# Column sums of four norms moved ahead of the last chunk that leads to them, the experts' residual inside the last V group, and weights split at other places

## The chip, the cores and the metric

The kernel runs on one core of one Trainium2 chip. The metric is the device time of one execution in microseconds (us). The engines are TensorE (PE; its weight loads are PEld), VectorE (DVE), ScalarE (ACT), GpSimd (POOL) and SyncE (SP), which issues nearly all transfers.

## The reference, cut to what matters

Two layers work on 512 prompt tokens and 32 sample tokens (T = 544) of width 1024:

```python
mod = silu(c) @ w_ada[l] + b_ada[l]               # sh1, sc1, g1, sh2, sc2, g2
h = rmsnorm(x, norm_mix_g[l]) * (1 + sc1) + sh1
y = mix_even(h, ...) if l % 2 == 0 else mix_odd(h, ...)
x = x + g1 * y
h = rmsnorm(x, norm_ffn_g[l]) * (1 + sc2) + sh2
x = x + g2 * peer(h, wq[l], k1[l], k2[l], u[l], v[l])
...
return rmsnorm(x, final_g), ...                   # and the new states
```

`mix_even` (layer 0) runs a GLU, a depthwise convolution with 31 taps, a LayerNorm and a swish over 512 channels, and causal means over 2, 4, 8 and 16 tokens with a linear map over the other 512; both feed one output projection. `mix_odd` (layer 1) is a short gated convolution between two projections. `peer` takes, per token and head, the best 16 of 128 x 128 experts: `sum_k g_k * gelu(u_k . h) * v_k`. The kernel computes gelu(U h) for all 16384 experts and multiplies by gates that are zero where an expert wasn't picked.

## The kernel before, in words

**Layout.** Everything is feature-major. X and H are [128, 8 chunks, 544] in f32. A product in f32 precision is made from f16 halves: each operand is split in a high part and a low part (value minus high part), and three matmuls (high by high, high by low, low by high; `PASSES`) accumulate in f32. A chunk of 128 output features takes 8 x 3 x 2 = 48 matmuls of 272 columns. PSUM is cut into four pairs of banks that are handed round (`begin` waits until the pair's last reader is done); for the first uses only three go round.

**Weights.** A slot of 128 x 4096 f32 comes into `raw[lane]` (two lanes), ACT makes its high part (`high`, L865), DVE its low part (`low`, L1193). Before that, ACT waits for the slot's transfer and until PE is done with every use of PSUM so far, so that `parts[lane]` is free. SP starts the next transfer into the lane when the low part is made.

**A norm.** ACT squares the chunks of X into H; PE multiplies them by a matrix of ones in f32 (`column_sums`, L613: for each chunk one matmul of 512 columns and one of 32, 32 records in all), which gives every partition the sum over features. DVE scales it into `stat` (L1162, `inverse_root`), ACT takes the inverse root (L849), DVE refines it in four steps (L1164 to L1167) and multiplies the eight chunks (L1172, `norm_x`), ACT modulates each (L856, `modulate`), and the result is split for the matmuls: ACT's copy to f16 (L870, `high_part`) and DVE's low part (L1200, `low_part`). ACT does all eight modulations before the eight copies. In norm 0 of layer 0 DVE makes both halves itself, chunk by chunk (L1249, L1251).

There are five norms: 0 at the start, 1 between layer 0's output projection and its queries, 2 between layer 0's experts and layer 1's input projection, 3 as 1 in layer 1, and 4 at the end (no modulation and no split; L1576 writes y). Ahead of norms 1 and 3, `project` (L580) makes eight chunks of the output projection with lane 0 for four and lane 1 for four; DVE adds each to X (`residual`, L1182), ACT squares (L1008).

**Ahead of norm 1, in layer 0.** The rest of `w_ada` is taken beside the input projection: 24 slots, each one call of `ada_rows(s)` on PE (L627, 16 records) into two buffers that the transfers refill (L404), and after every fourth an `ada_turn` (L637). DVE meanwhile does the convolution's 31 taps on two groups of two channel chunks (L1307, one instruction a tap and chunk); within the second group, after tap 10, the window sums, and after tap 24 the low halves of the four pool chunks (L1322) and the low part of lane 0's output weights. Pool chunk 3 takes the PSUM pair that chunk 0 leaves. ACT makes the high part of these weights after `take_rows(5)`, which waits for the last `ada_rows`.

**V phase.** A loop of 16 turns; a turn is two groups of 4 x 128 experts (`v_group`, L732), each eight chunks of 24 matmuls into one pair. DVE adds each chunk to ACC (L1539), and between the adds it splits the next weights and makes the next gated activations. After the last group `residual(l, "g2", True)` adds ACC times the gate to X (two instructions a chunk), and norm 2 or 4 follows. At the start of layer 1 both lanes' weights are split on ACT and DVE between the squares and the norm's first step.

Of the kernel before, what the change touches and what calls it, by code (L numbers as in the profile page):

```python
# [26 lines left out]
ALU = mybir.AluOpType  # L27
# [8 lines left out]
KD = D // P  # L36
# [35 lines left out]
FREE_FROM, LAST_FREE = 9, 14  # L72
CORNER = max(WINDOWS)
# [172 lines left out]
def build(nc, xT, vectors, state_a, state_b, state_c, w_pool, keys, whole_w, split_w, U, V,  # L246
          out_y, out_ap, out_as, out_bp, out_bs, out_cp, out_cs, gates_dram, act_dram, x_dram):
    with ExitStack() as ctx:
# [298 lines left out]
        def _(pe):  # L547
# [68 lines left out]

            def ada_rows(s):
# [104 lines left out]
            def v_group(lane, grp):  # L722

                pe.wait_ge(split[lane], lanes[lane].at(1))
                for c in range(KD):
                    u = begin("dve")
# [8 lines left out]
                    mm.then_inc(mm_done, 1)  # L735
                wts.n += 4
# [4 lines left out]
            for l in range(LAYERS):  # L741
                column_sums(begin("dve"), H, KD, sq_ready, NORM[2 * l] + 1)
                if l == 0:
                    for s in range(EARLY):
                        ada_rows(s)
# [18 lines left out]
                    for g in range(KA):  # L764
                        pool_branch(g)
                    for s in range(20, 2 * ADA_SLOTS):
                        ada_rows(s)
                        if s % 4 == 0:
                            ada_turn(s // 4 - 1)
                    ada_turn(2 * ADA_SLOTS // 4 - 1)  # L770
# [16 lines left out]
                    for m in range(4):  # L787
                        project(begin("dve"), 1, m, range(KD), True, True).then_inc(mm_done, 1)
                else:
# [4 lines left out]
                    for m in range(8):  # L794
# [4 lines left out]
                column_sums(begin("dve"), H, KD, sq_ready, NORM[2 * l + 1] + 1)  # L799
# [24 lines left out]
                with loop(pe, BODIES, *w.steps(dve=16), (lanes[0], 1), (lanes[1], 1), (wts, 8)):  # L824
# [4 lines left out]
            column_sums(begin("dve"), H, KD, sq_ready, NORM[4] + 1)  # L829
# [3 lines left out]
        def _(act):  # L833
# [32 lines left out]

            def high_part(src, dst, semaphore, value, signal):
                for k in range(KD):
                    act.wait_ge(semaphore, value + k)
                    act.copy(dst[:, 0, k, :], src[:, k, :]).then_inc(signal, 1)  # L870
# [51 lines left out]
            for l in range(LAYERS):  # L922
# [12 lines left out]
                else:  # L935
                    squares(X, H, KD, x_ready, 1)
                    for lane in range(2):
                        high(lane, U_SCALE)
                    root()
                    modulate(l, 0)  # L940
                    high_part(H, HM[l], h_ready, 2 * KD * l + 1, hm_high)
                if l == 0:
# [13 lines left out]
                    for g in range(KA):  # L956
                        take_pool(g)
                    take_turn(4)
                    take_rows(5)
                    high(0, 1.0)  # L960
# [41 lines left out]
                for half in range(2):  # L1002
# [134 lines left out]
        def _(dve):  # L1137
# [21 lines left out]
            def inverse_root(n, width):  # L1159

                u = next_use()
                dve.tensor_scalar(stat[:, 0, :], ps(u), 1.0 / width, EPS, ALU.mult, ALU.add).then_inc(dve_read, 1)  # L1162
# [11 lines left out]
            def residual(l, gate, experts):  # L1174
                for k in range(KD):
                    if experts:
                        pieces = [(ACC[:, k, a:b], a, b, s) for a, b, s in SEG]
                    else:
                        v = ps_halves(next_use())
                        pieces = [(v[:, 0, :], 0, HALF, 0), (v[:, 1, 0:NP_ - HALF], HALF, NP_, 0), (v[:, 1, NP_ - HALF:HALF], NP_, T, 1)]  # L1180
                    for y, a, b, s in pieces:
                        ins = dve.scalar_tensor_tensor(out=X[:, k, a:b], in0=y, scalar=mod[:, l, mod_at[gate] * KD + k, s:s + 1],  # L1182
# [468 lines left out]
```

## Time and profile before

| what | value |
|---|---|
| median of three runs | 3772.31 us (3771.55 to 3772.61) |
| profiled execution, its time | 3770.65 us |
| profiled execution, its span | 3768.9 us |
| TensorE's granted clock, mean | 0.983 of full speed |
| PE busy | 3627.0 us, 96% of the span |
| DVE busy | 2586.1 us, 69% |
| ACT busy | 1027.2 us, 27% |

The span is the time from the first to the last instruction of the profiled execution; its own time is 1.75 us more. PE is busy nearly throughout, so what matters are the few stretches where it is not.

### The profile page before, as it was taken

Reading aid. Unit: us, or ns where it says so; the run is one execution under the profiler, and the core shown is the slowest. Engines: PE = TensorE matmul, PEld = TensorE weight load, DVE = VectorE, ACT = ScalarE, POOL = GpSimd, SP = SyncE. Lnnn points to the kernel's source line nnn. Section 1 sums busy time; section 2 is a strip of 40 time slices with the busy share of each in tenths; the row PEclk is TensorE's granted clock in tenths of the full one; section 3 lists DMA queues with packets and bytes.
Section 4 is the critical chain, followed back from the end, with each engine's and each line's share of the span. In section 5 each row is a group of like instructions: output and inputs, shape, how many; then the busy total and the mean of one; then the engine's idle time right before and its main releaser. Section 6 shows DMA issues by size and latency. Waiting matters only on the chain.

```text
span 3768.9 us, 72843 instructions
## 1 busy us (share of the span) xinstructions
PE 3627.0 (96%) x31816; PEld 2959.8 (79%) x31816; DVE 2586.1 (69%) x3938; ACT 1027.2 (27%) x922; POOL 11.9 (0%) x34
## 2 busy tenths in 40 slices
PE   7778999999999999999979899999999999999998
PEld 3357888888888888888845688888888888888886
DVE  4857755556665888888734585555666488888886
ACT  3034333343332111111132333243343411111111
POOL 0000000000000000000000000000000000000000
PEclk9889999999999999999989999999999999999999
DMA  8732245454558454545312213464554775454540
GB/s 339 315 119 76 92 160 193 172 194 174 190 203 312 184 195 192 198 184 197 135 67 90 103 68 137 161 203 158 195 197 167 247 278 198 184 195 187 203 184 35
DMA packets 196225, 667.12 MB, mean 177 GB/s; under 512 B 11952, under 2 KB 151360, under 8 KB 152512
## 3 DMA queue, kind: packets, MB, share of 16 engines
q1 hardware_dynamic: 190608, 663.67, 47.3%
q8 instruction: 159, 2.61, 0.3%
q10 hardware_dynamic: 5392, 0.56, 0.1%
q14 instruction: 34, 0.28, 0.0%
q0 software_dynamic: 32, 0.01, 0.0%
HBM read 514.72 MB, written 149.49 MB: 176 GB/s over the span
## 4 chain that ended last, share of the span: by engine, by line
PE 92%; DVE 4%; DMA 3%; ACT 1%; issue 0%; SPq 0%; DVEq 0%; ACTq 0%
PE PS L732 38%; PE PS L688 35%; PE PS L663 5%; PE PS L600 4%; PE PS L718 3%; PE PS L580 2%; PE PS L613 1%; PE PS L627 1%; DMA ring<-whole_w 1%; DMA arena<-gates_dram 1%; PE PS L676 1%; ACT H L856 1%; DVE ring L1193 1%; PE PS L595 1%; DMA arena<-act_dram 1%; DVE arena L1307 1%
## 5 line engine op out<-in xcount | busy, mean ns | idle before, releaser
L688 PE MATMUL PS<-X,ring 128*128 128x272 f16 x12288 | 1437.0, 279 | 0.0
L732 PE MATMUL PS<-arena,ring 128*128 128x272 f16 x12288 | 1423.7, 279 | 2.6 <-DVE ring L1193 2.6
L732 PEld LDWEIGHTS PS<-arena,ring 128*128 128x128 f16 x12288 | 1202.2, 98 | 224.1 <-issue 3.2
L688 PEld LDWEIGHTS PS<-X,ring 128*128 128x128 f16 x12288 | 1198.8, 98 | 218.7 <-issue 0.4
L1193 DVE SCALAR_TENSOR_TENSOR ring<-ring 128x4096 f16<-128x4096 f32 x149 | 659.0, 4424 | 637.5 <-ACT ring L865 628.9
L865 ACT ACTIVATE ring<-ring 128x4096 f16<-128x4096 f32 x149 | 538.5, 3615 | 1154.8 <-PE PS L732 1119.3
L1539 DVE TENSOR_TENSOR ACC<-PS,ACC 128x544 f32<-128x544 f32 x512 | 363.1, 719 | 236.0 <-PE PS L732 236.0
L1035 ACT ACTIVATE H<-PS 128x544 f32<-128x544 f32 x256 | 159.7, 624 | 974.6 <-PE PS L688 974.5
L1529 DVE TENSOR_TENSOR arena<-arena 128x544 f32<-128x544 f32 x256 | 292.6, 1143 | 45.7 <-DMA arena<-act_dram 45.7
L663 PE MATMUL PS<-X,ring 128*128 128x272 f16 x1536 | 186.4, 282 | 29.4 <-DVE X L1200 29.4
L663 PEld LDWEIGHTS PS<-X,ring 128*128 128x128 f16 x1536 | 149.4, 99 | 63.5 <-issue 35.1
L1533 DVE TENSOR_TENSOR arena<-arena 128x544 f16<-128x544 f32 x256 | 185.8, 726 | 8.7
L600 PE MATMUL PS<-arena,ring 128*128 128x512 f16 (+1 forms) x1152 | 141.4, 279 | 22.0 <-DVE arena L1200 22.0
L600 PEld LDWEIGHTS PS<-arena,ring 128*128 128x128 f16 x1152 | 70.7, 96 | 92.6 <-issue 24.5
L1057 ACT COPY ACC<-PS 128x1024 f32<-128x1024 f32 x136 | 131.4, 1016 | 23.5 <-PE PS L718 23.5
L718 PE MATMUL PS<-arena 128*128 128x128 f16 x2176 | 136.4, 218 | 0.0
L718 PEld LDWEIGHTS PS<-arena 128*128 128x128 f16 x2176 | 130.5, 97 | 2.6
L1482 DVE TENSOR_TENSOR arena<-pairs,arena 128x2048 f16<-128x2048 f16 x68 | 83.1, 1222 | 67.5 <-PE PS L718 67.1
L1531 DVE CAST arena<-arena 128x544 f16<-128x544 f32 x256 | 113.7, 444 | 8.8
L580 PE MATMUL PS<-ACC,ring 128*128 128x272 f16 x768 | 94.0, 286 | 14.4 <-DVE ring L1193 7.1
L580 PEld LDWEIGHTS PS<-ACC,ring 128*128 128x128 f16 x768 | 76.7, 100 | 31.3 <-DVE ACC L1346 7.2
L1307 DVE SCALAR_TENSOR_TENSOR arena<-arena,vec 128x574 f32<-128x574 f32 x120 | 87.7, 814 | 0.0
(149 smaller groups left out, 1538.1 us busy)
## 6 DMA issues: line engine op xcount, KB each, us to landing
ring<-U SPq DMA_DIRECT2D x64, 2048.0 KB, 10.6
ring<-V SPq DMA_DIRECT2D x64, 2048.0 KB, 7.6
act_dram<-H SPq DMA_DIRECT2D x64, 1088.0 KB, 5.0
gates_dram<-ACC SPq DMA_DIRECT2D x68, 1024.0 KB, 5.7
arena<-gates_dram SPq DMA_DIRECT2D x32, 2176.0 KB, 9.5
arena<-act_dram SPq DMA_DIRECT2D x64, 1088.0 KB, 5.0
ring<-split_w SPq DMA_DIRECT2D x17, 2048.0 KB, 9.0
arena<-whole_w SPq DMA_DIRECT2D x11, 2048.0 KB, 10.9
```

What stands on the lines that cost most here:

```text
L580: mm = pe.matmul(ps_halves(u)[:, half, :], parts[lane][:, pw, k * 512 + m * P:k * 512 + (m + 1) * P], Z16[:, ph, k, half * HALF:(half + 1) ...
L600: mm = pe.matmul(ps(u)[:, a:b], parts[lane][:, pw, k * 512 + m * P:k * 512 + (m + 1) * P], HM[l][:, ph, k, a:b], start=(k == n == 0), stop ...
L663: mm = pe.matmul(ps_halves(u)[:, half, :], parts[lane][:, pw, k * 512 + c % 4 * P:k * 512 + (c % 4 + 1) * P], H16[:, ph, k, half * HALF:(h ...
L688: mm = pe.matmul(ps_halves(u)[:, half, :], parts[lane][:, pu, k * 512 + j * P:k * 512 + (j + 1) * P], H16[:, ph, k, half * HALF:(half + 1) ...
L718: mm = pe.matmul(ps(u, 1024)[:, i * P:(i + 1) * P], E2[:, buf, b, :, e], G1[:, buf, n, b, :, e], start=(n == 0), stop=(n == 1))
L732: mm = pe.matmul(ps_halves(u)[:, half, :], parts[lane][:, pv, j * D + c * P:j * D + (c + 1) * P], WT[:, grp, pw, j, half * HALF:(half + 1) ...
L865: act.activation(parts[lane][:, 0, :], raw[lane], ACT.Copy, scale=scale).then_inc(high_made[lane], 1)
L1035: act.activation(dst.rearrange("p (b c) -> p b c", b=2), ps_halves(u), ACT.Gelu_apprx_tanh, scale=1.0 / U_SCALE).then_inc(act_read, 1)
L1193: dve.scalar_tensor_tensor(out=parts[lane][:, 1, :], in0=raw[lane], scalar=scale, in1=parts[lane][:, 0, :], op0=ALU.mult, op1=ALU.subtract ...
L1529: dve.tensor_tensor(a, a, gate, ALU.mult).then_inc(wf_ready, 1)
L1533: dve.tensor_tensor(WT[:, grp, 1, j, :], a, WT[:, grp, 0, j, :], ALU.subtract).then_inc(w_ready, 1)
L1539: dve.tensor_tensor(acc, ps_halves(u), acc, ALU.add).then_inc(dve_read, 1)
```

## The change

1. `output_tail` takes the last two chunks of the output projection together with the norm's sums: chunk 6, then the sums of five chunks of squares (`EARLY_SUMS`), then chunk 7, then the other three. The sums are taken as two halves of 272 columns. `v_group` does the same around its last chunk in the last group of a layer, for norms 2 and 4; PE's loop is one turn shorter and its last turn is written out.
2. The experts' residual is done per chunk inside the last V group (`experts`), one chunk behind the adds.
3. DVE makes both halves of the split in all norms (`split_part`), each chunk as soon as it is modulated; ACT's `high_part` is gone.
4. Lane 1's next weights are split before norms 1 and 3 (ACT's `high` before `root`, DVE's `low` before `norm_x`) and not behind them. At layer 1's start lane 0's are split inside the last V group and lane 1's behind the split of H.
5. In layer 0's convolution the pool's low halves are made after taps 14 (three) and 19 (the fourth), and lane 0's low part after tap 22. PE takes pool chunk 3 between `ada_rows(21)` and `ada_rows(22)`, and ACT makes lane 0's high part ahead of `take_rows(5)`.

```diff
+            def norm_sums(u, norm, ks):
+                for k in ks:
+                    pe.wait_ge(sq_ready, NORM[norm] + 1 + k)
+                    for half in range(2):
+                        mm = pe.matmul(ps_halves(u)[:, half, :], ones[:, :], H[:, k, half * HALF:(half + 1) * HALF],
+                                       start=(k == 0), stop=(k == KD - 1))
+                if ks[-1] == KD - 1:
+                    mm.then_inc(mm_done, 1)
+
+            def output_tail(norm):
+                u6, u7, us = (begin("dve") for _ in range(3))
+                project(u6, 1, 2, range(KD), True, True).then_inc(mm_done, 1)
+                norm_sums(us, norm, range(EARLY_SUMS))
+                project(u7, 1, 3, range(KD), True, True).then_inc(mm_done, 1)
+                norm_sums(us, norm, range(EARLY_SUMS, KD))
...
-            def v_group(lane, grp):
+            def v_group(lane, grp, norm=None):
...
-                    u = begin("dve")
+                    if norm is None or c < 6:
+                        u = begin("dve")
+                    elif c == 6:
+                        u, u7, us = (begin("dve") for _ in range(3))
+                    else:
+                        norm_sums(us, norm, range(EARLY_SUMS))
+                        u = u7
...
+                if norm is not None:
+                    norm_sums(us, norm, range(EARLY_SUMS, KD))
...
-                    for g in range(KA):
+                    for g in range(KA - 1):
                         pool_branch(g)
-                    for s in range(20, 2 * ADA_SLOTS):
-                        ada_rows(s)
-                        if s % 4 == 0:
-                            ada_turn(s // 4 - 1)
-                    ada_turn(2 * ADA_SLOTS // 4 - 1)
+                    ada_rows(20)
+                    ada_turn(4)
+                    ada_rows(21)
+                    pool_branch(KA - 1)
+                    ada_rows(22)
+                    ada_rows(23)
+                    ada_turn(5)
...
-                column_sums(begin("dve"), H, KD, sq_ready, NORM[2 * l + 1] + 1)
+                output_tail(2 * l + 1)
...
-                with loop(pe, BODIES, ...):
+                with loop(pe, BODIES - 1, ...):
                     from_turn_before("dve")
                     for grp in range(2):
                         v_group(grp, grp)
                 from_turn_before("dve")
+                v_group(0, 0)
+                v_group(1, 1, 2 * l + 2)
...  (ACT)
                     squares(X, H, KD, x_ready, 1)
-                    for lane in range(2):
-                        high(lane, U_SCALE)
                     root()
                     modulate(l, 0)
-                    high_part(H, HM[l], h_ready, 2 * KD * l + 1, hm_high)
+                    high(1, U_SCALE)
...
-                    for g in range(KA):
+                    for g in range(KA - 1):
                         take_pool(g)
                     take_turn(4)
+                    take_pool(KA - 1)
+                    high(0, 1.0)
                     take_rows(5)
-                    high(0, 1.0)
                     take_turn(5)
...
+                high(1, U_SCALE)
                 root()
                 modulate(l, 1)
-                act.wait_ge(x_stored, 16 * (l + 1))
-                high_part(H, H16, h_ready, 2 * KD * l + KD + 1, h_high)
-                high(1, U_SCALE)
...
+                if l + 1 < LAYERS:
+                    high(0, U_SCALE)
                 w.take("dve", KD)
...  (DVE)
-            def low_part(src, dst, signal_high, signal):
+            def split_part(src, dst, made, signal_high, signal):
                 for k in range(KD):
+                    dve.wait_ge(h_ready, made + k + 1)
+                    dve.tensor_copy(dst[:, 0, k, :], src[:, k, :]).then_inc(signal_high, 1)
                     dve.wait_ge(signal_high, l * KD + k + 1)
                     dve.tensor_tensor(dst[:, 1, k, :], src[:, k, :], dst[:, 0, k, :], ALU.subtract).then_inc(signal, 1)
...
-                    for lane in range(2):
-                        low(lane, U_SCALE)
                     norm_x(4)
-                    low_part(H, HM[l], hm_high, hm_split)
-                    for lane in (0, 1, 0, 1):
+                    split_part(H, HM[l], 2 * KD * l, hm_high, hm_split)
+                    for lane in (1, 0, 1, 0, 1):
                         low(lane, U_SCALE)
...
-                            if first == 2 and i == 24:
-                                for g in range(KA):
+                            if first == 2 and i in (14, 19):
+                                for g in range(KA - 1) if i == 14 else (KA - 1,):
...
+                            if first == 2 and i == 22:
                                 low(0, 1.0)
...
-                residual(l, "g1", False)
+                residual(l)
+                low(1, U_SCALE)
                 norm_x((3, 5)[l])
-                low_part(H, H16, h_high, h_split)
-                low(1, U_SCALE)
+                dve.wait_ge(x_stored, 16 * (l + 1))
+                split_part(H, H16, 2 * KD * l + KD, h_high, h_split)
...
+                def experts(k, ahead):
+                    dve.wait_ge(dve_read, w.dve.at(ahead))
+                    for a, b, s in SEG:
+                        ins = dve.scalar_tensor_tensor(out=X[:, k, a:b], in0=ACC[:, k, a:b],
+                                                       scalar=mod[:, l, mod_at["g2"] * KD + k, s:s + 1],
+                                                       in1=X[:, k, a:b], op0=ALU.mult, op1=ALU.add)
+                    ins.then_inc(x_ready, 1)
...
+                        if not more:
+                            if c == 0:
+                                dve.wait_ge(x_back, 16 * (l + 1))
+                            else:
+                                experts(c - 1, -1)
+                            if l + 1 < LAYERS and c == 2:
+                                low(0, U_SCALE)
...
-                dve.wait_ge(x_back, 16 * (l + 1))
-                dve.wait_ge(dve_read, w.dve.at())
-                residual(l, "g2", True)
+                experts(KD - 1, 0)
+                dve.wait_ge(x_ready, KD * (l + 1))
```

## Rows read from the trace of the kernel before

**Rows 1.** The page: chain by engine; one group of matmuls (xcount | busy us, mean ns).
```profile
PE 92%; DVE 4%; DMA 3%; ACT 1%; issue 0%; SPq 0%; DVEq 0%; ACTq 0%
...
L688 PE MATMUL PS<-X,ring 128*128 128x272 f16 x12288 | 1437.0, 279 | 0.0
```

**Rows 2.** Waits of PE over the span: us in total, times, longest.
```profile
PE PS L663 <- DVE X L1200: 29.4, 2, 14.7
PE PS L600 <- DVE arena L1200: 22.0, 1, 22.0
PE PS L646 <- DVE ACC L1322: 15.2, 1, 15.2
```

**Rows 3.** Timeline, 134 to 264 us: start, us, what [idle before <-releaser].
```profile
154.78 20.44 DVE L1307 SCALAR_TENSOR_TENSOR arena<-arena,vec 128x574 f32<-128x574 f32 x28
...
156.47 4.36 PE L646 MATMUL PS<-arena,wpool 128*128 128x512 f32 x12
...
184.99 0.35 SPq L404 DMA_DIRECT2D arena<-whole_w  x1
...
194.53 1.92 PE L627 MATMUL PS<-arena,keyT 128*32 128x512 f32 x16 [1.56 <-DMA arena<-whole_w]
...
200.65 4.42 DVE L1193 SCALAR_TENSOR_TENSOR ring<-ring 128x4096 f16<-128x4096 f32 x1 [20.77 <-ACT ring L865]
204.99 8.81 DVE L1307 SCALAR_TENSOR_TENSOR arena<-arena,vec 128x574 f32<-128x574 f32 x12
...
205.33 7.78 PE L580 MATMUL PS<-ACC,ring 128*128 128x272 f16 x48 [7.05 <-DVE ring L1193]
...
217.46 2.88 DVE L1330 SCALAR_TENSOR_TENSOR arena<-PS,arena 128x512 f32<-128x512 f32 x8 [3.66 <-PE PS L613]
```

**Rows 4.** Timeline of norm 1, 262 to 312 us.
```profile
271.45 8.73 PE L613 MATMUL PS<-H,ones 128*128 128x512 f32 x32
...
272.72 0.66 ACT L1008 ACTIVATE H<-X 128x544 f32<-128x544 f32 x1 [4.91 <-DVE X L1182]
...
280.29 0.72 DVE L1162 TENSOR_SCALAR stat<-PS 128x544 f32<-128x544 f32 x1 [7.61 <-PE PS L613]
...
284.50 5.17 DVE L1172 TENSOR_TENSOR H<-X,stat 128x544 f32<-128x544 f32 x8
...
302.36 0.62 ACT L1024 ACTIVATE arena<-PS 128x544 f32<-128x544 f32 x1 [1.03 <-PE PS L663]
```

**Rows 5.** Timeline of norm 2, 1870 to 1960 us.
```profile
1896.47 0.72 DVE L1539 TENSOR_TENSOR ACC<-PS,ACC 128x544 f32<-128x544 f32 x1 [2.06 <-PE PS L732]
1897.31 6.69 DVE L1182 SCALAR_TENSOR_TENSOR X<-ACC,mod,X 128x512 f32<-128x512 f32 x16
...
1899.06 10.50 PE L613 MATMUL PS<-H,ones 128*128 128x512 f32 x32 [2.70 <-ACT H L843]
...
1904.60 7.11 ACT L865 ACTIVATE ring<-ring 128x4096 f16<-128x4096 f32 x2
...
1908.31 8.76 DVE L1193 SCALAR_TENSOR_TENSOR ring<-ring 128x4096 f16<-128x4096 f32 x2 [4.31 <-ACT ring L865]
...
1916.98 0.72 DVE L1162 TENSOR_SCALAR stat<-PS 128x544 f32<-128x544 f32 x1
...
1940.01 0.62 ACT L986 ACTIVATE arena<-PS 128x544 f32<-128x544 f32 x1 [5.53 <-PE PS L600]
```

**Rows 6.** Timeline of norm 4, 3715 us to the end.
```profile
3742.83 0.72 DVE L1539 TENSOR_TENSOR ACC<-PS,ACC 128x544 f32<-128x544 f32 x1 [2.06 <-PE PS L732]
...
3751.07 1.28 ACT L849 ACT_TABLE_LOAD   x1
...
3756.09 0.72 DVE L1162 TENSOR_SCALAR stat<-PS 128x544 f32<-128x544 f32 x1 [5.73 <-PE PS L613]
```

**Rows 7.** Norm 0's split on DVE: L1251 alone (ns min/median/max, first and last start); timeline from 35 us.
```profile
L1251 DVE TENSOR_TENSOR ACC<-H,ACC x8: 724/726/726, 43.6 to 51.4; 128x544 f16<-128x544 f32 x8
...
52.16 12.46 PE L600 MATMUL PS<-ACC,ring 128*128 128x512 f16 x102 [0.23 <-DVE ACC L1251]
```

More of the change, by code:

```diff
@@ L72 @@
 FREE_FROM, LAST_FREE = 9, 14
+EARLY_SUMS = 5
 CORNER = max(WINDOWS)
@@ L741, in _ @@
             for l in range(LAYERS):
-                column_sums(begin("dve"), H, KD, sq_ready, NORM[2 * l] + 1)
                 if l == 0:
+                    column_sums(begin("dve"), H, KD, sq_ready, NORM[0] + 1)
                     for s in range(EARLY):
@@ L786, in _ @@
                     split_ready(1)
-                    for m in range(4):
+                    for m in range(2):
                         project(begin("dve"), 1, m, range(KD), True, True).then_inc(mm_done, 1)
@@ L793, in _ @@
                         project_chunk(1, c // 4 % 2, c, (lambda k: pe.wait_ge(hm_split, KD + k + 1)) if c == 0 else None)
-                    for m in range(8):
+                    for m in range(6):
                         if m % 4 == 0:
@@ L823, in _ @@
                 drained()
-                with loop(pe, BODIES, *w.steps(dve=16), (lanes[0], 1), (lanes[1], 1), (wts, 8)):
+                with loop(pe, BODIES - 1, *w.steps(dve=16), (lanes[0], 1), (lanes[1], 1), (wts, 8)):
                     from_turn_before("dve")
@@ L828, in _ @@
                 from_turn_before("dve")
-            column_sums(begin("dve"), H, KD, sq_ready, NORM[4] + 1)
+                v_group(0, 0)
+                v_group(1, 1, 2 * l + 2)
         @block.scalar
@@ L865, in high @@
                 act.activation(parts[lane][:, 0, :], raw[lane], ACT.Copy, scale=scale).then_inc(high_made[lane], 1)
[L867 to L870, printed above, removed]
             def store_state(dst, src):
@@ L1161, in inverse_root @@
                 u = next_use()
-                dve.tensor_scalar(stat[:, 0, :], ps(u), 1.0 / width, EPS, ALU.mult, ALU.add).then_inc(dve_read, 1)
+                if n <= 2:
+                    dst, sums = stat[:, 0, :], ps(u)
+                else:
+                    dst, sums = stat[:, 0, :].rearrange("p (b c) -> p b c", b=2), ps_halves(u)
+                dve.tensor_scalar(dst, sums, 1.0 / width, EPS, ALU.mult, ALU.add).then_inc(dve_read, 1)
                 dve.wait_ge(std_ready, n)
@@ L1172, in norm_x, with residual @@
                     dve.tensor_tensor(H[:, k, :], X[:, k, :], stat[:, 2, :], ALU.mult).then_inc(xn_ready, 1)
-            def residual(l, gate, experts):
+            def residual(l):
                 for k in range(KD):
[L1176 to L1180, printed above, removed]
+                    v = ps_halves(next_use())
+                    pieces = ((v[:, 0, :], 0, HALF, 0), (v[:, 1, 0:NP_ - HALF], HALF, NP_, 0), (v[:, 1, NP_ - HALF:HALF], NP_, T, 1))
                     for y, a, b, s in pieces:
-                        ins = dve.scalar_tensor_tensor(out=X[:, k, a:b], in0=y, scalar=mod[:, l, mod_at[gate] * KD + k, s:s + 1],
+                        ins = dve.scalar_tensor_tensor(out=X[:, k, a:b], in0=y, scalar=mod[:, l, mod_at["g1"] * KD + k, s:s + 1],
                                                        in1=X[:, k, a:b], op0=ALU.mult, op1=ALU.add)
-                    ins.then_inc(x_ready if experts else dve_read, 1)
-                    if k == KD // 2 - 1 and not experts:
+                    ins.then_inc(dve_read, 1)
+                    if k == KD // 2 - 1:
                         low(0, U_SCALE)
-                dve.wait_ge(x_ready if experts else dve_read, KD * (l + 1) if experts else w.dve.at())
+                dve.wait_ge(dve_read, w.dve.at())
             def low(lane, scale):
@@ L1246, in _ @@
                     scale_part(0, 0).then_inc(mod_ready, 1)
-                    for k in range(KD):
-                        dve.wait_ge(h_ready, k + 1)
-                        dve.tensor_copy(HM[0][:, 0, k, :], H[:, k, :]).then_inc(hm_high, 1)
-                        dve.wait_ge(hm_high, k + 1)
-                        dve.tensor_tensor(HM[0][:, 1, k, :], H[:, k, :], HM[0][:, 0, k, :], ALU.subtract).then_inc(hm_split, 1)
+                    split_part(H, HM[0], 0, hm_high, hm_split)
                     low(1, U_SCALE)
@@ L1547, in add_and_prepare @@
                             low(lane, 1.0)
+                        if not more:
+                            if c == 0:
+                                dve.wait_ge(x_back, 16 * (l + 1))
+                            else:
+                                experts(c - 1, -1)
+                            if l + 1 < LAYERS and c == 2:
+                                low(0, U_SCALE)
                         if more and c in (1, 3, 5, 6):
```

## The prediction, made before the changed kernel ran

> **What bounds the kernel now.** I read the page's chain first: 92% of it is PE's own work [rows 1]. An f16 matmul of 272 columns costs 1437.0 / 12288 = 0.117 us, and the change takes away none of these. So it can gain only where PE stands still. PE's waits come next [rows 2]: 29.4 us in two waits ahead of the queries (norms 1 and 3), 22.0 us ahead of layer 1's input projection (norm 2), 15.2 us behind the pool chunks in layer 0. Then I read the timelines of these places and of the end, and in each asked which engine ends last and what stands in its queue.
>
> In layer 0's convolution [rows 3] PE is not the one to watch. DVE runs 28 taps in 20.44 us (0.73 each) to 175.2, then stands 20.77 us for ACT's high part of the output weights, then does the last 12 taps to 213.8. Only then are LayerNorm's sums complete (L1330 at 217.46). ACT was late because its high part was queued behind the last row of `w_ada`, which was queued on PE behind pool chunk 3, which waited for DVE at tap 24. It is a ring of waits, and DVE's hole is its price. In norm 1 [rows 4] PE is busy to 280.05 and all that follows is a serial chain on DVE and ACT; the first chunk of queries is done at 302.36, that is 22.07 us after L1162 starts. Norm 3 repeats this to 0.1 us. In norm 2 [rows 5] the sums end at 1909.56 but L1162 starts only at 1916.98: DVE has two low parts in the way.
>
> **The change part by part.**
>
> *Layer 0's convolution.* Nothing is removed; the work is put in another order. After the window sums DVE has 40 taps (29.25 us), four pool halves (2.9) and one low part (4.35), 36.5 us from 154.78 on if nothing is waited for: it ends at 191.3, not 213.8. Are the inputs there? Pool chunks 0 to 2 leave PE at 160.83 [rows 3]; DVE comes to them after 8 taps, at 160.6, and the last is on ACT until 161.6: no wait. PE goes on with row 20 (1.92 us), the turn (1.05), row 21 (the queue is empty from 163 on, so its slot is there) and pool chunk 3, done at 166.9; DVE asks for it at 170.1. ACT's high part (3.6) is done at 171.4; DVE asks at 175.2. PE's own order: row 21's end at 165.9 starts the last transfer, and one such took 194.53 - 184.99 = 9.5 us [rows 3], so the last row runs at 175.4, its turn at 179, and the 48 matmuls of L580, which took 7.78 in a cold start [rows 3], end at 187.4. Two sums follow, to 189.6; the last one waits for the last tap and ends at 192.7. L1330 starts at 192.85 for 217.46: **-24.6**. Unknown is the last transfer: PE has some 2 us to spare; 5 us later would leave -20.5. The other end is -25.2.
>
> *Sums in halves.* Eight chunks took 8.6 us, 1.08 each [rows 4]. The trace has no f32 matmul of 272 columns. The upper bound is 1.08; the lower is four times the f16 price for 544 columns, 4 x 0.234 = 0.94. I take 0.95, as the 32-column records are short against their weight loads.
>
> *Norms 1 and 3.* The reorder alone saves PE nothing, since PE was busy from the projection to the end of the sums. Call T the time at which the projection ended before (271.45). Now five sums precede chunk 7, so it ends at T + 4.75. Its residual is done 1.27 later and its square 0.6 after that (ACT goes on to the next instruction somewhat before the end) [rows 4], at T + 6.6. Only then, on ACT in order, comes lane 1's high part, 3.6 us, and on DVE, ahead of `inverse_root`, its low part, 4.34 in a row of two (from 1908.31 to 1916.98 for two) [rows 5]. L1162 starts at T + 14.65; before it was T + 8.84. **+5.8.** PE's last three sums end at T + 7.7, so they hide only a third of this. Before, this pair was done behind the queries' first chunk, where PE had lane 0's four chunks to work on: it was free. In return, the split no longer waits for eight modulations and eight copies on ACT. DVE multiplies to L1162 + 9.28 (284.50 - 280.29 + 8 x 0.634) [rows 4]. Then copy and low part alternate: the low part starts 0.48 after the copy, and the pace is (51.4 - 43.6) / 7 = 1.11 us a chunk, as in norm 0 [rows 7]. The last starts at L1162 + 17.55, PE may read it 0.78 later (52.16 for 51.38) and needs 0.7: the first chunk is taken by ACT at L1162 + 19.13, where it was 22.07. **-2.9.** Each of these norms: 5.8 - 2.9 = **+2.9**, both together +5.8 (2.7 each with sums at 0.94, 3.5 at 1.08). ACT modulates at 1.02 a chunk from L1162 + 5, so it stays ahead of DVE; X's store lands some 7.5 us after it starts, ahead of the split that overwrites it.
>
> *Norm 2.* PE's last two V chunks and the sums: chunk 6 ended at 1893.6 (7's end, 1896.4, less 24 matmuls). DVE, in the last group, adds a chunk every 2.78 us (0.72) and now does the residual of the one before (6.69 / 8 = 0.84 [rows 5]). Lane 0's low part after add 2 holds it from 1884.0 to 1888.4. The backlog (adds 3, 4 and 5) is gone by 1892.9. PE asks for the pair of chunk 4 at 1890.85 and it is free at 1890.6: no stall, with 0.25 us to spare. The five squares are there. Sums to 1898.4, chunk 7 to 1901.15, its add, then the residuals of 6 and 7, which both stand behind add 7, to 1903.55, square 7 to 1904.3, last sum to 1905.4. L1162 would start at 1905.65. Here the clock may fall: after PE's wait of 2.70 the same 32 records took 10.50, not 8.73 [rows 4, 5], and now there is a wait of 2.3 us in two pieces. I add 0.35 and keep 1.85 as the end: L1162 at 1906.0 for 1916.98, -11.0. The two high and low parts are off the path: lane 0's lies in the last group, lane 1's is made at 1925 to 1930 and needed after four chunks, at 1943. The split then gives 23.03 - 19.15 = -3.9. Together **-14.9** (-15.3 to -13.4).
>
> *Norm 4.* The same without weights and without a split: chunk 7 ends at 3747.5 for 3742.76, add 7 at 3747.6, square 7 done at 3750.6, last sum at 3751.75, L1162 at 3752.3 with 0.3 for the clock, for 3756.09 [rows 6]. **-3.8** (-4.2 to -2.2).
> The table load for the root takes 1.28 us [rows 6] and now follows square 7 from 3750.6 to 3751.9, just ahead of L1162's end. The Trainium skill ("ScalarE: Activation LUTs", "What ACT_TABLE_LOAD costs") puts a switch of sets at about 2.66 us, drain included. By that rule the root would start about 0.5 later in norms 2 and 4, and the sum would be -36.5; no row here shows the drain on the path.
>
> *The loop's last turn written out* costs nothing by my count: the U phase is straight code too, and runs at 0.117 us a matmul [rows 1].
>
> Sum: -24.6 + 5.8 - 14.9 - 3.8 = **-37.5 us**. The profiled execution took 3770.65 us, 1.75 more than its span and 1.66 less than the median of 3772.31. Against its own time the sum gives 3733.2; against the median, **3734.8**.
>
> **The rivals.**
> *A. Slower: PE starves in the written-out V groups.* They hold 2 x 768 = 1536 matmuls that used to come from the loop's code. From 0.117 + 37.5 / 1536 = 0.141 us each, the whole gain is gone; at 0.15 the kernel takes 3786. Against it stand the 12288 straight ones of the U phase. 2 in 100.
> *B. The weights of lane 1 aren't on the path of norms 1 and 3* (if ACT's and DVE's work on them overlapped the sums). Then L1162 starts at T + 7.9, and each norm gives -0.9 - 2.9 = -3.8 in place of +2.9: sum -50.9, 3721. Against it: ACT's wait for PSUM's last use, chunk 7 included, and both queues' order. 6 in 100.
> *C. The ring of waits in layer 0 opens less*: the last rows of `w_ada` become PE's limit because two transfers share the queue, or the waits come back at pool chunk 3. With the last row 12 us later the gain there is some -13.5: sum -26.4, 3746. For it: PE waited for both last slots before. Against: DVE needs neither of them. 10 in 100.
> *D. The low part inside the last V group stalls PE.* The margin of 0.25 us is thin; with DVE 3 us later, PE stands 2.8: 3737.6. 10 in 100.
> *E. What is saved is lost again in the same place* (within 0.2%, which is about what a measurement of this kernel can tell from no change). Only several of the above together would do it. 2 in 100.
>
> **How the numbers follow.** My forecast has 70 in 100 and gives 3734.8. Its bounds: the best ends of the terms are -25.2 + 5.4 - 15.3 - 4.2 = -39.3, the worst -20.5 + 7.0 - 13.4 - 2.2 = -29.1, so 3733 to 3743 by the named unknowns alone. B lies below, C above. I let the range go from 3728 to 3743: it covers the forecast with errors of a few us in the starts, and D; A, B, C and E are left out. Faster by over 0.2% (below 3764.8): 0.96; within: 0.02; slower: 0.02.
>
> **What would show each step.** DVE's wait at L1193 of 20.77 us is gone and L1330 starts near 193. PE's wait ahead of the queries becomes longer, not shorter: from the sums' end at T + 7.7 to L1162 + 10.6 = T + 25.2, some 17.5 us for 14.7, with L865 and L1193 between the last square and L1162. PE's wait ahead of layer 1 falls from 22.0 to about 11 us. If L865 of lane 1 runs before the last square, B holds. If PE's L732 shows waits in the last group, D or A does. The prediction fails most easily if the last transfer of `w_ada` is slow or if the price of the lane's split is hidden by something I don't see.

## The result and the profile after

| | time before, us | time after, us |
|---|---|---|
| median | 3771.93 (3771.26 to 3772.61, 4 runs) | 3735.89 (3734.07 to 3737.14, 4 runs) |
| profiled execution, its span | 3768.9 | 3733.2 |
| granted clock, mean | 0.983 | 0.986 |

The ratio is 0.9904, with a 95% interval of 0.9887 to 0.9921. The forecast was 3734.8 with a range of 3728 to 3743.

The waits of PE over the span of the changed kernel (us in total, times, longest), to compare with [rows 2]:

```profile
PE PS L682 <- DVE X L1227: 34.9, 3, 17.3
...
PE PS L601 <- DVE arena L1227: 11.0, 2, 10.7
PE PS L646 <- DMA arena<-whole_w: 10.7, 3, 7.2
```

The wait ahead of layer 1 has halved (10.7 us for 22.0). The two ahead of the queries are longer than before, 17.3 us each for 14.7, in a kernel that is 36 us faster. The pool chunk's wait of 15.2 is gone; PE now waits there for slots of `w_ada`, 1.6 to 3.3 us each (the longest such wait, 7.2, comes before this stretch and was there before, at 7.0). The timeline of layer 0's convolution in the changed kernel (for [rows 3]):

```profile
155.90 5.90 DVE L1328 SCALAR_TENSOR_TENSOR arena<-arena,vec 128x574 f32<-128x574 f32 x8
...
165.59 1.92 PE L646 MATMUL PS<-arena,keyT 128*32 128x512 f32 x16 [1.62 <-DMA arena<-whole_w]
...
169.36 3.61 ACT L895 ACTIVATE ring<-ring 128x4096 f16<-128x4096 f32 x1
...
176.12 4.42 DVE L1218 SCALAR_TENSOR_TENSOR ring<-ring 128x4096 f16<-128x4096 f32 x1
177.50 3.64 PE L646 MATMUL PS<-arena,keyT 128*32 128x512 f32 x16 [1.89 <-DMA arena<-whole_w]
180.45 11.71 DVE L1328 SCALAR_TENSOR_TENSOR arena<-arena,vec 128x574 f32<-128x574 f32 x16
...
183.56 7.39 PE L581 MATMUL PS<-ACC,ring 128*128 128x272 f16 x48 [0.59 <-ACT mod L916]
...
190.78 4.41 PE L614 MATMUL PS<-arena,ones 128*128 128x512 f32 x16
195.31 2.87 DVE L1352 SCALAR_TENSOR_TENSOR arena<-PS,arena 128x512 f32<-128x512 f32 x8 [3.14 <-PE PS L614]
```

DVE's low part no longer stands behind an idle stretch, and the taps end at 192.2. But the last row of `w_ada` starts at 177.5, the first 48 matmuls of the output projection follow at 183.56, and PE's sums end 3 us after DVE's last tap. Norm 1 (timeline, for [rows 4]):

```profile
244.12 4.75 PE L623 MATMUL PS<-H,ones 128*128 128x272 f32 x20
...
254.27 3.16 PE L623 MATMUL PS<-H,ones 128*128 128x272 f32 x12
...
255.53 0.66 ACT L1032 ACTIVATE H<-X 128x544 f32<-128x544 f32 x1 [9.49 <-DVE X L1207]
...
256.10 3.60 ACT L895 ACTIVATE ring<-ring 128x4096 f16<-128x4096 f32 x1
...
259.81 4.42 DVE L1218 SCALAR_TENSOR_TENSOR ring<-ring 128x4096 f16<-128x4096 f32 x1 [4.31 <-ACT ring L895]
264.15 0.72 DVE L1190 TENSOR_SCALAR stat<-PS 128x544 f32<-128x544 f32 x1
...
283.44 0.62 ACT L1046 ACTIVATE arena<-PS 128x544 f32<-128x544 f32 x1 [6.15 <-PE PS L682]
```

Between the sums' end and the norm's first step (L1190) lie lane 1's high part and low part, and nothing else is done there. Norm 2 (timeline, for [rows 5]):

```profile
1874.60 0.72 DVE L1562 TENSOR_TENSOR ACC<-PS,ACC 128x544 f32<-128x544 f32 x1 [0.92 <-PE PS L757]
...
1881.69 1.08 PE L623 MATMUL PS<-H,ones 128*128 128x272 f32 x4
...
1882.60 1.73 DVE L1568 SCALAR_TENSOR_TENSOR X<-ACC,mod,X 128x512 f32<-128x512 f32 x4
...
1884.25 2.10 PE L623 MATMUL PS<-H,ones 128*128 128x272 f32 x8 [1.48 <-ACT H L873]
...
1886.46 0.72 DVE L1190 TENSOR_SCALAR stat<-PS 128x544 f32<-128x544 f32 x1 [2.13 <-PE PS L623]
...
1905.80 0.62 ACT L1010 ACTIVATE arena<-PS 128x544 f32<-128x544 f32 x1 [2.68 <-PE PS L601]
```

The step starts 2.1 us behind the last residual's end, where it was 13. PE stands 1.48 us for square 6. In norm 4 the first step is at 3720.43 for 3756.09.

If the span is cut at LayerNorm's first instruction and at each norm's first step and the ACT instruction that takes the first chunk behind it, the 35.7 us between the two profiled executions fall like this (all from the starts of the rows shown and of their like in norms 3 and 4):

| stretch | forecast | measured |
|---|---|---|
| start to LayerNorm's first instruction | -24.6 | 195.31 - 217.46 = -22.15 |
| from there to norm 1's first step | +5.8 | 68.84 - 62.83 = +6.0 |
| norm 1's step to the first chunk of queries | -2.9 | 19.29 - 22.07 = -2.8 |
| from there to norm 2's first step | -11.0 | 1603.02 - 1614.62 = -11.6 |
| norm 2's step to the first chunk of layer 1 | -3.9 | 19.34 - 23.03 = -3.7 |
| from there to norm 3's first step | +5.8 | 192.49 - 186.88 = +5.6 |
| norm 3's step to the first chunk of queries | -2.9 | 19.29 - 22.07 = -2.8 |
| from there to norm 4's first step | -3.8 | 1602.85 - 1607.13 = -4.3 |

### The profile page after: what moved, and what is told of

Same layout as the page of the kernel before. It is cut to its first block, busy times and chain, and to the rows that moved or that the text cites. A ratio compares the mean times of both kernels' runs of the same rounds, so it can differ in the third digit from the quotient of the medians.

```text
span 3733.2 us, 72787 instructions
## 1 busy us (share of the span) xinstructions
PE 3621.0 (97%) x31816; PEld 2962.5 (79%) x31816; DVE 2594.7 (70%) x3962; ACT 1014.6 (27%) x898; POOL 11.9 (0%) x34
## 4 chain that ended last, share of the span: by engine, by line
PE 93%; DVE 3%; DMA 2%; ACT 0%; issue 0%; SPq 0%; DVEq 0%; ACTq 0%
PE PS L757 38%; PE PS L707 37%; PE PS L682 5%; PE PS L601 4%; PE PS L737 3%; PE PS L581 2%; PE PS L646 1%; DMA arena<-whole_w 1%; DMA ring<-whole_w 1%; PE PS L695 1%; PE PS L623 1%; PE PS L596 1%; DVE H L1200 0%; DMA arena<-gates_dram 0%; DVE ring L1218 0%
## 5 line engine op out<-in xcount | busy, mean ns | idle before, releaser
L757 PE MATMUL PS<-arena,ring 128*128 128x272 f16 x12288 | 1424.1, 279 | 2.3 <-DVE ring L1218 1.2
L757 PEld LDWEIGHTS PS<-arena,ring 128*128 128x128 f16 x12288 | 1202.0, 98 | 224.3 <-issue 2.9
## 6 DMA issues: line engine op xcount, KB each, us to landing
ring<-U SPq DMA_DIRECT2D x64, 2048.0 KB, 10.4
```

What stands on the lines that cost most here:

```text
L757: mm = pe.matmul(ps_halves(u)[:, half, :], parts[lane][:, pv, j * D + c * P:j * D + (c + 1) * P], WT[:, grp, pw, j, half * HALF:(half + 1) ...
```

## The experiments

The theory has four effects. Two are gains from a new order: the ring of waits in layer 0 is opened, and the splits and the residual leave the path in norms 2 and 4. One is a gain because DVE makes both halves of the split. One is a loss: lane 1's weights stand ahead of norms 1 and 3. The trace of the changed kernel adds a sharper form: PE's work is the same wherever the sums stand, so the early sums, the change's first point, should be worth nothing or less. The rivals are in the expectations. All experiments start from the changed kernel. Differences in us are between medians; those of the kernel before lie between 3770.45 and 3772.4 in the sessions in which it was timed beside these runs, so a difference of 1 to 2 us between runs of different sessions says little.

### Lane 1's weights behind norms 1 and 3 again

```diff
-                high(1, U_SCALE)
                 root()
                 modulate(l, 1)
+                high(1, U_SCALE)
...
                 residual(l)
-                low(1, U_SCALE)
                 norm_x((3, 5)[l])
...
                 split_part(H, H16, 2 * KD * l + KD, h_high, h_split)
+                low(1, U_SCALE)
```

> The changed kernel, but lane 1's next weights are split behind norms 1 and 3 again (ACT's high part after modulate, DVE's low part after split_part). My theory: in the changed kernel L1190 of norm 1 starts 9.85 us after the projection's end (264.15 for 254.3), because the last square is followed by 3.6 us on ACT and 4.34 on DVE; without them it starts 0.25 after the sums, at 3.1. So each of the two norms gives back 6.75 us, together -13.5: about 3722.4 us, a ratio of 0.9964 to the changed kernel. The rival (the pair overlaps the sums and costs nothing; or what it costs ahead of the norm it saves behind it, where DVE would be the limit again): within 3 us of the changed kernel, 3736.

Measured: 3721.86 us (3719.67 to 3722.99), ratio to before 0.9869 (0.9854 to 0.9884): 14.0 us under the changed kernel. Its timeline at norm 1:

```profile
252.00 3.16 PE L623 MATMUL PS<-H,ones 128*128 128x272 f32 x12
...
253.27 0.66 ACT L1032 ACTIVATE H<-X 128x544 f32<-128x544 f32 x1 [9.49 <-DVE X L1207]
...
255.27 0.72 DVE L1190 TENSOR_SCALAR stat<-PS 128x544 f32<-128x544 f32 x1 [2.04 <-PE PS L623]
...
268.33 3.60 ACT L895 ACTIVATE ring<-ring 128x4096 f16<-128x4096 f32 x1
...
273.47 4.42 DVE L1218 SCALAR_TENSOR_TENSOR ring<-ring 128x4096 f16<-128x4096 f32 x1
...
274.57 0.62 ACT L1046 ACTIVATE arena<-PS 128x544 f32<-128x544 f32 x1 [2.64 <-PE PS L682]
```

The step follows the projection's end by 3.3 us, where it was 9.9, and DVE's 4.42 us now run while PE works on lane 0's chunks. From LayerNorm's first instruction to norm 1's step it took 61.85 us for 68.84, and from layer 1's first chunk to norm 3's step 185.89 for 192.49. The pair costs 6.6 to 7.0 us in each norm and buys nothing behind it: the first chunk still comes 19.30 us behind the step. The rival is out.

### Layer 0's order of before

```diff
-                    for g in range(KA - 1):
+                    for g in range(KA):
                         pool_branch(g)
-                    ada_rows(20) ... pool_branch(KA - 1) ... ada_turn(5)
+                    (the loop of before)
...
-                    take_pool(KA - 1)
-                    high(0, 1.0)
                     take_rows(5)
+                    high(0, 1.0)
...
-                            if first == 2 and i in (14, 19):   # and the low part at 22
+                            if first == 2 and i == 24:         # all four, and the low part
```

> The changed kernel, but with layer 0's order of before: all four pool chunks in a row on PE, the pool's low halves and lane 0's low part after tap 24, ACT's high part behind take_rows(5). My theory (a ring of waits in which DVE stood 20.8 us): that hole is back, and the time rises by 22 to 24 us: 3758.9 us. The rival (the gain in layer 0 comes from elsewhere, such as transfers that start sooner): less than half of it, 3747 or under.

Measured: 3758.09 us (3756.94 to 3759.56), ratio to before 0.9966 (0.9952 to 0.9979), 22.2 us over the changed kernel. DVE's timeline shows the hole again:

```profile
178.93 0.79 DVE L1340 SCALAR_TENSOR_TENSOR ACC<-PS,vec,ACC 128x544 f16<-128x544 f32 x1 [1.80 <-ACT ACC L937]
200.70 4.43 DVE L1215 SCALAR_TENSOR_TENSOR ring<-ring 128x4096 f16<-128x4096 f32 x1 [20.98 <-ACT ring L893]
205.04 8.81 DVE L1325 SCALAR_TENSOR_TENSOR arena<-arena,vec 128x574 f32<-128x574 f32 x12
```

So six tenths of the whole gain of 36 us come from the change's fifth point.

### One link of the ring closed again

```diff
-                    high(0, 1.0)
                     take_rows(5)
+                    high(0, 1.0)
```

> The changed kernel, with one instruction of layer 0's new order undone: ACT's high part of lane 0's output weights comes behind take_rows(5) again; the pool's low halves stay at taps 14 and 19. My theory of a ring of waits: the last row ends at 181.1, the high part at 185.5, DVE's low part at 189.9, sixteen taps at 201.5; L1352 starts near 202.8 for 195.3, +7.5: 3743.4 us. If the place of the high part were the whole cause, all 22 us would be back (3758); if only the pool's place mattered, none (3736).

Measured: 3743.15 us (3740.27 to 3744.51), ratio to before 0.9922 (0.9908 to 0.9936): +7.3. The timeline from 160 us:

```profile
179.56 0.58 ACT L910 COPY keyT<-PS 128x512 f32<-128x512 f32 x1 [11.77 <-PE PS L646]
180.04 3.62 ACT L895 ACTIVATE ring<-ring 128x4096 f16<-128x4096 f32 x1
...
183.69 4.43 DVE L1218 SCALAR_TENSOR_TENSOR ring<-ring 128x4096 f16<-128x4096 f32 x1 [8.84 <-ACT ring L895]
188.04 11.72 DVE L1328 SCALAR_TENSOR_TENSOR arena<-arena,vec 128x574 f32<-128x574 f32 x16
```

DVE waits 8.84 us in place of none. With ACT's place undone a third of the 22.2 us is lost and two thirds stay, so ACT's place isn't the whole cause. The opposite run, with ACT's place kept and the pool's undone, wasn't made: whether the pool's place is enough to close the ring by itself is open.

### ACT makes the high halves again

```diff
                     modulate(l, 0)
+                    high_part(H, HM[l], h_ready, 2 * KD * l + 1, hm_high)
...
                 modulate(l, 1)
+                act.wait_ge(x_stored, 16 * (l + 1))
+                high_part(H, H16, h_ready, 2 * KD * l + KD + 1, h_high)
...
-                split_part(...)
+                low_part(...)
```

> The changed kernel, but ACT makes the high halves of the split in norms 1 to 3 after all eight modulations, as before. My theory: the first chunk of matmuls ends 22.07 us and not 19.2 behind the norm's first step in norms 1 and 3, and 23.0 and not 19.3 in norm 2: +2.9, +3.7 and +2.9, together +9.5: 3745.4 us. The rival (PE at its lower clock after the gap is the limit for the first chunk, so that the earlier start buys nothing): within 2 us of 3735.9.

Measured: 3743.36 us (3742.59 to 3747.96), ratio to before 0.9928 (0.9915 to 0.9942): +7.5 by the medians. In the trace the first chunk of queries is taken 22.40 us behind norm 1's step, and 22.14 behind norm 3's, layer 1's 22.12 behind norm 2's, for 19.29, 19.29 and 19.34: +8.7 in sum. Most of the +9.5 is there, and the rival's 0 to 2 is out.

```profile
263.29 0.72 DVE L1198 TENSOR_SCALAR stat<-PS 128x544 f32<-128x544 f32 x1
...
285.69 0.62 ACT L1054 ACTIVATE arena<-PS 128x544 f32<-128x544 f32 x1 [4.89 <-PE PS L682]
```

### All sums behind the last chunk

```diff
                 project(u6, 1, 2, range(KD), True, True).then_inc(mm_done, 1)
-                norm_sums(us, norm, range(EARLY_SUMS))
                 project(u7, 1, 3, range(KD), True, True).then_inc(mm_done, 1)
-                norm_sums(us, norm, range(EARLY_SUMS, KD))
+                norm_sums(us, norm, range(KD))
...  (and the same in v_group)
```

> The changed kernel, but all eight sums come behind the last chunk, in all four norms; everything else stays. My theory: five sums ahead of the last chunk take nothing off the path, since PE has the same work and is busy until the sums end; they only delay the last chunk by 4.6 us, and in norms 1 and 3 what hangs on it is later than the sums. So norms 1 and 3 give 4.6 us each and norms 2 and 4, where PE waits 1.5 us for square 6 and would no longer, 1.8 each: -12.8, 3723.1 us. The rival (the early sums shorten the tail behind the last chunk, which is what the order looks made for): the tail is longer by five sums in each of four norms, up to +18 us, 3754.

Measured: 3724.2 us (3721.64 to 3727.05), ratio to before 0.9877 (0.9862 to 0.9892): -11.7. Norm 1's step comes 63.88 us after LayerNorm's first instruction for 68.84, norm 2's 1601.53 after the chunk before it for 1603.02, and the other two likewise: -5.0, -1.5, -4.6, -1.8, together -12.8. The eight sums take 7.50 us in one piece (timeline at norm 1), and what hangs on the last chunk runs beside them:

```profile
248.69 7.50 PE L623 MATMUL PS<-H,ones 128*128 128x272 f32 x32
248.89 1.03 DVE L1205 SCALAR_TENSOR_TENSOR X<-PS,mod,X 128x272 f32<-128x272 f32 x3 [4.52 <-PE PS L581]
...
250.52 3.60 ACT L893 ACTIVATE ring<-ring 128x4096 f16<-128x4096 f32 x1
...
254.23 4.42 DVE L1216 SCALAR_TENSOR_TENSOR ring<-ring 128x4096 f16<-128x4096 f32 x1 [4.30 <-ACT ring L893]
258.57 0.72 DVE L1188 TENSOR_SCALAR stat<-PS 128x544 f32<-128x544 f32 x1
```

The early sums are not neutral in the changed kernel; they cost some 12 us.

### Both at once, and three early sums

The first has both edits shown above; the second has lane 1's weights behind and one constant changed:

```diff
-EARLY_SUMS = 5
+EARLY_SUMS = 3
```

> Both at once: lane 1's weights split behind norms 1 and 3, and all eight sums behind the last chunk in four norms. My theory: the two aren't additive. With the weights out of the way PE's sums are the last thing in norms 1 and 3, and their order is worth nothing there (4.6 us each in the run with the sums alone); norms 2 and 4 still give 1.8 each. From 3721.9 with the weights alone: -3.6, 3718.3 us. If the two were additive (each removing a wait of its own): 3735.9 - 14.0 - 11.7 = 3710.2. If early sums had been good for something once the weights are gone: above 3722.

> Lane 1's weights behind norms 1 and 3, and three sums ahead of the last chunk in place of five. My theory: in norms 2 and 4 PE then has sums 3 to 5 left (2.75 us) while the residual and square of chunk 6 are made (2.7 us behind the chunk's end), so it never waits, and the norm's first step starts as soon as with no early sum: the same as with all sums behind, 3718.3 us, within 1. If early sums cost by themselves, it lies between that run and 3721.9.

Measured: 3719.12 us (3717.36 to 3720.84), ratio to before 0.9858 (0.9843 to 0.9874), and 3719.17 (3716.41 to 3721.72), 0.9862 (0.9847 to 0.9877). The two edits are not additive (3710.2 would be 9 us lower), and no early sum and three are the same. Against five early sums with the weights behind (3721.86) the times alone settle nothing, as the intervals overlap. In the traces both reach norm 3's step 185.6 us after the chunk before, against 185.9 with five early sums; both lead to norm 4's step in 1601.1, against 1602.85. Norm 2 alone gave 1.4 and 1.7. So once the weights are out of the way, five early sums cost 1.4 to 1.8 us in each of norms 2 and 4, 0.2 in norm 3, and nothing clear in norm 1.

### The residual in one piece behind the last add

```diff
-                            else:
-                                experts(c - 1, -1)
...
-                experts(KD - 1, 0)
+                for k in range(KD):
+                    experts(k, 0)
```

> The kernel with lane 1's weights and all sums behind, and the experts' residual done in one piece behind the last add of both layers, as before the change (lane 0's low part stays inside the last V group). It prices the residual's place by itself. In the kernel before, norm 4's first step came 13.26 us behind the last add; with the residual inside the group and all sums behind it came 7.33 us behind. My theory: PE waits 2.7 us for the first square, is fed one square per 0.83 us and runs part of the sums at its lower clock, so the step comes some 12.5 us behind the last add in norms 2 and 4: +5.2 each, 3719.1 + 10.4 = 3729.5 us. So of the 11.6 us that norm 2's first step gained, only about 4 are the residual's and the sums', the rest the two lanes' splits. The rival (the residual could have stayed behind, as PE's sums hide it at 0.92 a chunk for 0.84): within 3 us of 3719.1.

Measured: 3726.81 us (3725.7 to 3730.35), ratio to before 0.9884 (0.9867 to 0.99): +7.7 to the run with both edits, for the +10.4 expected. The first step of norm 2 and norm 4 in its timeline:

```profile
1883.17 0.72 DVE L1188 TENSOR_SCALAR stat<-PS 128x544 f32<-128x544 f32 x1 [4.37 <-PE PS L623]
...
3701.23 0.72 DVE L1560 TENSOR_TENSOR ACC<-PS,ACC 128x544 f32<-128x544 f32 x1 [2.06 <-PE PS L755]
3701.99 6.69 DVE L1566 SCALAR_TENSOR_TENSOR X<-ACC,mod,X 128x512 f32<-128x512 f32 x16
...
3703.71 9.29 PE L623 MATMUL PS<-H,ones 128*128 128x272 f32 x32 [2.59 <-ACT H L871]
...
3713.11 0.73 DVE L1188 TENSOR_SCALAR stat<-PS 128x544 f32<-128x544 f32 x1 [4.43 <-PE PS L623]
```

Norm 4's step comes 11.88 us behind the last add; I had 12.5. The 32 records took 9.29 us behind the wait, with the granted clock at 0.50 from 3705 to 3708 us, and 7.50 at 1.00 without a wait. From the chunk before, norm 4's step takes 1605.64 us for 1601.10 in the run with both edits, norm 2's 1605.66 (1883.17 less 277.51) for 1601.76: +4.5 and +3.9.

With the kernel before, this run and the run with both edits, norms 2 and 4 can be taken apart. Norm 4: 1607.13 before, 1605.64 with the halved sums all behind the last chunk and the residual behind the last add, 1601.10 with the residual inside the group, 1602.85 with five early sums. Norm 2: 1614.62, 1605.66, 1601.76 and 1603.02 in the same order, where the first difference, 9.0 us, holds the two lanes' splits besides.

### High halves on both engines

```diff
                     modulate(l, 0)
+                    act.wait_ge(h_ready, 3 * KD)
+                    high_part(H, HM[l])              # chunks 4 to 7, signals act_high
...  (the same behind modulate(l, 1))
+                    if k < own:                      # own: 4, in norm 0 all 8
                         dve.tensor_copy(dst[:, 0, k, :], src[:, k, :]).then_inc(signal_high, 1)
...
+                    else:
+                        split_acts[0] += 1
+                        dve.wait_ge(act_high, split_acts[0])
```

> The kernel with lane 1's weights and all sums behind, and in norms 1 to 3 ACT makes the high halves of chunks 4 to 7 behind its modulations while DVE makes those of 0 to 3. DVE then has 4 copies less, 0.48 us each, so its last low half starts 1.9 us sooner. My theory: PE's lower clock at the start of the first chunk (three to four steps at 1.36 us) now sets most of its end, and only about 1 us a norm is gained: -3, against -5.7 if DVE were the only limit, and 0 if the clock already was.

Measured: 3715.08 us (3714.53 to 3720.41), ratio to before 0.9852 (0.9839 to 0.9866). That is faster than both kernels. Against the run without this edit (3719.12 us, 0.9858) it is 4.0 us by the medians, but the intervals overlap; by the traces the queries' first chunk is taken 0.36 us sooner behind norm 1's step and 0.13 behind norm 3's, and layer 1's 0.10 later behind norm 2's, 0.4 us in all. DVE's last low half at norm 1 did start sooner, 15.9 us behind the step for 17.6, but PE hadn't got there. The row of DVE's last four low halves at norm 1, and the windows there (us, busy time of PE, PEld, DVE, ACT, POOL, then the granted clock), show why:

```profile
272.28 2.63 DVE L1241 TENSOR_TENSOR X<-H,X 128x544 f16<-128x544 f32 x4 [0.15 <-ACT X L897]
...
268.94:273.00 4.06, 4.06 (x19) 2.63 (x20) 3.80 (x8) 3.97 (x9) 0.00 (x0) 0.50 0.00 0
273.00:275.00 2.00, 2.00 (x17) 1.61 (x16) 1.92 (x4) 2.00 (x3) 0.00 (x0) 0.87 0.00 0
275.00:277.00 2.00, 2.00 (x20) 1.70 (x18) 0.00 (x0) 2.00 (x1) 0.00 (x0) 1.00 0.00 0
```

PE is busy throughout, and stands at 0.50 of its clock, the lower of its two levels (1.2 GHz), for the first 4 us behind a wait of 10.7. With DVE out of the way, PE's clock sets the first chunk at norm 1.

## Why the prediction was right, point by point

**Layer 0's convolution** (forecast -24.6, measured -22.15; undone +22.2). The ring of waits was real. DVE's side came as worked out: from the 8 taps' start at 155.90 to the last tap at 192.2 are 36.3 us for 36.5. The term was mis-sized on PE's side. The prediction had row 21's slot there when PE came; it wasn't. PE stood 1.62 us for it (row at 165.59), and that also put off the last transfer. The last row started at 177.5, not 175.4, and ran at the lower clock (0.50 granted from 178 to 180 us, 3.64 us, not 1.92), so that PE and not DVE ended last. Some 1.1 us of the delay are the profiled execution's own: it reached the taps at 155.90 for 154.78, from instructions that the change doesn't touch.

**Norms 1 and 3** (forecast +5.8 and -2.9 each; measured +6.0 and +5.6, -2.8 twice). That the weights' place costs more ahead of the step than the split gives behind it is shown: taking the pair away gave 14.0 us. That the reorder alone saves PE nothing was right but too mild: it costs. The sums cost 0.92 us a chunk in halves (4.58 us for five, from 244.28 to 248.87 on the chain), a little under the 0.94 that the prediction called the lower bound. Two small slips of the prediction's own sums don't matter: with 0.94 the norm gives 2.85 and not 2.7, and its addends for the first chunk (17.55, 0.78, 0.7) make 19.03 and not 19.13, where 19.29 was measured.

**Norm 2** (-14.9; measured -15.3). The step at norm 2 gained 11.6. By the stretches above, the residual's place gave 3.9 and the early sums took back 1.3; the other 9.0 are the weights' splits and the halved sums. As everything but the splits gave 1.5 in norm 4, some 7.5 are the splits' (by arithmetic; no run moved the splits alone).

**Norm 4** (-3.8; measured -4.3). The clock's allowance of 0.3 wasn't needed: in norm 2 sums 6 and 7 ran in 2.10 us behind a wait of 1.48, at a granted clock of 1.00, which it also was in norm 4. The gain is the residual's (4.5) and the halved sums' (1.5), less 1.75 for the early sums. Here and in norm 2, L1190's end and the root lie 0.03 to 0.04 us apart, with the table load ended 0.9 us before the root:

```profile
3719.01 1.28 ACT L879 ACT_TABLE_LOAD   x1
3720.43 0.72 DVE L1190 TENSOR_SCALAR stat<-PS 128x544 f32<-128x544 f32 x1 [2.13 <-PE PS L623]
3721.18 0.66 ACT L879 ACTIVATE stat<-stat 128x544 f32<-128x544 f32 x1 [0.90 <-DVE stat L1190]
```

The load starts at 3719.01 and the root at 3721.18, 2.17 us later. The Trainium skill ("ScalarE: Activation LUTs", "What ACT_TABLE_LOAD costs") has about 2.66 us for a switch; by the row it was done within 2.17, so the half microsecond that the rule would add isn't there.

**The rivals.** A (the written-out groups starve PE) is out: L757 still takes 0.117 us a matmul, in the last group too. Its price was mis-stated: the written-out turns hold 4 x 192 = 768 matmuls, not 1536, so the gain would have been gone from 0.166 us each. B is out by the order of the rows (the high part at 256.10 follows the last square at 255.53) and by the first experiment. C happened in small: PE is the last by 3 us, and the loss is 2.5. D is out: PE runs through the last V group of layer 0 without a wait, and the add of chunk 6 comes six times 2.79 us behind that of chunk 0 (1874.60 for 1857.87), so the margin of 0.25 us held.

```profile
1854.82 19.67 PE L757 MATMUL PS<-arena,ring 128*128 128x272 f16 x168
```

By the spans the forecast promised 1.8 us too much: 2.5 in layer 0 and 0.3 in norm 1, less 1.0 by which norms 2, 3 and 4 gave more than forecast. The mechanisms hold, but that the total is this close is in part misses of opposite sign.

What stays open: why the last row of `w_ada` starts between 175.8 and 177.5 us from execution to execution, whether the pool's place alone opens the ring, and whether the halves on both engines are worth more than the 0.4 us that the traces show.

## What to carry to other kernels

Moving work of an engine that is busy to the end of a stretch shortens nothing: ask first what hangs on each result, and put the result with the longest tail first. Here this was the last chunk, and the sums, or all but three, belonged behind it. A split of weights that is free behind a norm cost 6.6 to 7.0 us of its 8.0 ahead of it, because both of its engines are in the norm's chain. And the largest idle time of an engine that isn't the bottleneck (DVE's 20.8 us) can be the whole price of a ring of waits; closing one of its links again brought back a third.

## What the runs showed of the hardware that was not expected

The lower clock behind a wait has a price. In the last kernel PE ran the first 4 us at 0.50 behind the wait of 10.7 us, and this sets the first chunk at norm 1; where DVE makes all the halves, its last low half does (in the run with both edits PE stands 0.24 us for it at 278.15, 1 us before the chunk is taken). The 32 records of sums took 9.29 us behind a wait of 2.59, partly at 0.50, and 7.50 without one; sums 6 and 7 behind 1.48 us ran at 1.00.

Executions of some of the faster kernels lie further apart than those of before: 3714.53 to 3720.41 in five runs of the last one, 3769.86 to 3773.32 in all 29 of before. In the traces much of this is layer 0: LayerNorm's first instruction starts at 193.4 to 197.1 us in eight kernels with the same code up to there, where the two with the old order have 217.46 and 217.42. That DVE's wait absorbed such differences before, and that PE's clock and the last transfers are on the path now, fits the rows but wasn't tested.
